# A table of paces with lighter first slots, Gelu ahead of the copy of sums, a tile's end in six pieces, score loads by ScalarE

## The chip, the cores and the metric

One Trainium2 chip, one core of it. The time is the device time of one execution in microseconds; less is better. The kernel before took 4760.69 us in the median of three runs (4751.96 to 4765.37).

## The reference

One layer of an encoder for 1152 tokens (1024 of a prompt, 8 sequences of 16 new ones), all in fp32: normalization and modulation, one input projection, a gated linear attention (gla) and a stick-breaking attention, their merge, a residual with normalization, and then a retrieval of single-neuron experts. The last part takes most of the time:

```python
q = (h @ peer_wq).reshape(n, PEER_HEADS, 2, PEER_HALF)
s = jnp.einsum('nhpd,hpkd->nhpk', q, peer_keys)
sc, ix = lax.top_k(s, PEER_TOPK)                       # 16 of 128, two halves, 8 heads
cand = sc[:, :, 0, :, None] + sc[:, :, 1, None, :]
top, pos = lax.top_k(cand.reshape(...), PEER_TOPK)     # 16 of 256
eid = jnp.take_along_axis(cid, pos, axis=-1)
g = jax.nn.softmax(top, axis=-1)
act = jax.nn.gelu(jnp.einsum('nhkd,nd->nhk', peer_u[eid], h))
return jnp.einsum('nhk,nhkd->nd', g * act, peer_v[eid])
```

Each token picks 128 of 16384 experts, so 1152 x 128 rows of 4 KB are read from `peer_u` and as many from `peer_v`, 1.2 GB in all.

## The kernel before

The 1152 tokens are nine tiles of 128, in three groups of three tiles (`GROUPS`). For each group the program goes through six stages: norm, stick, gla, mix, res, select. Select computes the scores of all three tiles and chooses the experts of the first; the scores of the two others go to DRAM.

Beside the stages, from the select of group 0 on, runs the retrieval (`Peer`), cut into **slots**. There are 128 slots for a tile. In slot s GpSimd fetches one row of `peer_u` for each of the 128 tokens (`fetch_u`, L2424, 0.524 MB, an indirect DMA into one of seven buffers; the first tile alone uses the fourteen of both rings), VectorE multiplies it by the token's vector and sums it (`dot`, L2595), one slot for one expert of every token. A tile later the same tile's values come: for 64 pairs of tokens GpSimd fetches the 128 rows of `peer_v` of each (`fetch_v`, L2432), and TensorE adds a pair with four products (`add_values`, L2494). So the first tile's slots fetch u alone, and from slot 138 on (`FIRST` = 10 in tile 1) both come, about 0.56 pairs a slot. After slot 1151 only values are left.

GpSimd has all fetches in one queue, in order of slots, six slots ahead. Before it fetches it waits until the buffer's last user is done: a dot (VectorE) or a pair (TensorE).

Between a tile's dots and its values lie these steps, at fixed slots k of the next tile: ScalarE's Gelu of the dots (`gelu`, k = 0), VectorE's product with the gates (`weigh`, L2607, `WEIGH_AT` = 2), the transpose of the weights on TensorE (k = 4), ScalarE's copy of it and the spreading of single weights (`set_alone`), and at k = 6 the transpose of the next ids. The sums of the tile before are copied out of PSUM by ScalarE in two halves (`keep_sums`, L2549); the second copy stands behind the last pair, at k = 125, so ahead of the next Gelu in ScalarE's queue. VectorE ends the tile (`finish`, L2613 to L2625) at `END_AT` = 9: gate, residual, normalization, scale and shift, in one go. The experts of the other two tiles of a group are chosen beside the slots (`choose_beside`), from scores that GpSimd loads (`load_beside`, L2291) in two halves; the second load waits until the fourth head is read.

What ties slots to stages is a list that `paces()` computes once: the stages call `K.tick(engine, beside)` at fixed places, 771 times on each of TensorE, VectorE and ScalarE, and the n-th tick runs the engine's part of the retrieval up to slot `slots[n]`. Within a group the slots from `128 * first - 14` up to the next group's are dealt out over its ticks in proportion to a weight for each. In the stick stage two ticks are one step, with one `sb_l` (L1158) and one `sb_z` (L1166) on VectorE.

## Time and profile before

| | us |
|---|---|
| median of three runs | 4760.69 |
| the profiled execution | 4755.65 |
| its span, first to last instruction | 4753.6 |
| TensorE busy | 3429.4 |
| VectorE busy | 2747.8 |
| GpSimd busy (issuing of gathers) | 2400.4 |
| ScalarE busy | 932.0 |

The three runs lie within 0.3% of each other. No single engine is busy throughout, and DMA moved 1580.58 MB at a mean of 333 GB/s. The span falls into five parts: group 0 alone to about 850 us; the select of group 0 and the stick stage of group 1, in which only u rows are fetched, to 1272; the rest of group 1 to 2115; group 2 to 3442; and the tail with the gathers alone. A share of the whole span is a mean over these, so the rows are read by part. A PE clock of 0.50 means 1.2 GHz, of 1.00 2.4 GHz.

### The profile page before, as it was taken

Reading aid. Unit: us, or ns where it says so; the run is one execution under the profiler, and the core shown is the slowest. Engines: PE = TensorE matmul, PEld = TensorE weight load, DVE = VectorE, ACT = ScalarE, POOL = GpSimd, SP = SyncE. Lnnn points to the kernel's source line nnn. Section 1 sums busy time; section 2 is a strip of 40 time slices with the busy share of each in tenths; the row PEclk is TensorE's granted clock in tenths of the full one; section 3 lists DMA queues with packets and bytes.
Section 4 is the critical chain, followed back from the end, with each engine's and each line's share of the span. In section 5 each row is a group of like instructions: output and inputs, shape, how many; then the busy total and the mean of one; then the engine's idle time right before and its main releaser. Section 6 shows DMA issues by size and latency. Waiting matters only on the chain.

```text
span 4753.6 us, 46576 instructions
## 1 busy us (share of the span) xinstructions
PE 3429.4 (72%) x16090; PEld 1698.1 (36%) x16090; DVE 2747.8 (58%) x6580; ACT 932.0 (20%) x2008; POOL 2400.4 (50%) x2390
## 2 busy tenths in 40 slices
PE   7989999878889799778898797897833333333355
PEld 4556754545445443334344364442400000000000
DVE  3443313789777554787776777446866576654420
ACT  3552300134422200114445232000100000000000
POOL 0000000235576555566776666465566666666665
PEclk8999999989998799889999898898955555555566
DMA  8775352678899999999999999899999999999998
GB/s 317 276 252 198 146 165 82 262 270 292 309 362 355 349 381 419 380 399 353 373 383 334 340 356 374 328 419 391 346 377 378 375 388 373 384 357 372 381 374 330
DMA packets 445319, 1580.58 MB, mean 333 GB/s; under 512 B 48328, under 2 KB 87624, under 8 KB 434720
## 3 DMA queue, kind: packets, MB, share of 16 engines
q0 software_dynamic: 342544, 1297.77, 71.2%
q1 hardware_dynamic: 100640, 278.20, 15.9%
q8 instruction: 131, 2.15, 0.2%
q10 hardware_dynamic: 1904, 1.65, 0.1%
q14 instruction: 100, 0.82, 0.0%
HBM read 1527.99 MB, written 49.43 MB: 332 GB/s over the span
## 4 chain that ended last, share of the span: by engine, by line
PE 35%; DVE 19%; POOL 17%; issue 10%; DMA 10%; another core or an unknown queue 6%; ACT 3%; SPq 0%; PEld 0%; DVEq 0%; ACTq 0%; PEldq 0%; POOLq 0%
POOL peer_v_ring L2432 9%; POOL peer_u_ring L2424 7%; PE wide L1829 6%; DVE peer_u_ring L2595 5%; DMA peer_v_ring<-in_peer_v,expertsT 5%; PE wide L750 4%; PE bank L2494 4%; PE wide L2136 3%; PE wide L1401 3%; PE wide L1389 2%; DMA peer_u_ring<-in_peer_u,experts 2%; PE wide L815 2%; PE wide L760 1%; PE wide L796 1%
## 5 line engine op out<-in xcount | busy, mean ns | idle before, releaser
L2424 POOL DMA_INDIRECT peer_u_ring<-in_peer_u,experts x1089 | 1123.3, 1032 | 777.8 <-DVE peer_u_ring L2595 454.3
L2494 PE MATMUL bank<-peer_v_ring,peer_lone 128*32 128x512 f32 x4356 | 805.5, 811 | 888.3 <-DMA peer_v_ring<-in_peer_v,expertsT 705.2
L2432 POOL DMA_INDIRECT peer_v_ring<-in_peer_v,expertsT x1089 | 1096.7, 1007 | 592.0 <-issue 296.5
L2595 DVE SCALAR_TENSOR_TENSOR peer_u_ring<-peer_u_ring,wide 128x1024 f32<-128x1024 f32 x680 | 813.4, 1217 | 486.8 <-DMA peer_u_ring<-in_peer_u,experts 435.5
L2494 PEld LDWEIGHTS bank<-peer_v_ring,peer_lone 128*32 128x32 f32 x4356 | 110.2, 123 | 1440.3 <-issue 1403.6
L2595 DVE SCALAR_TENSOR_TENSOR peer_u_ring<-peer_u_ring,peer_h 128x1024 f32<-128x1024 f32 x409 | 490.7, 1218 | 25.8 <-SPq L271 15.9
L1401 PE MATMUL wide<-w_ring,hT 128*128 128x256 f32 x1152 | 268.2, 391 | 6.9 <-DVE gla_v L1726 6.9
L750 PE MATMUL wide<-hT,w_ring 128*128 128x384 f32 x768 | 267.4, 496 | 5.9 <-DVE sb_hide L2699 3.1
L2136 PE MATMUL wide<-mT,w_ring 128*128 128x384 f32 x768 | 266.1, 496 | 3.1 <-SPq L271 3.1
L2393 POOL MEMSET peer_lone<- 128x1087 f32 x1 | 1.0, 1003 | 488.3 <-SPq L271 488.3
L1401 PEld LDWEIGHTS wide<-w_ring,hT 128*128 128x128 f32 x1152 | 221.5, 195 | 69.8 <-issue 39.2
L1865 DVE TENSOR_TENSOR mix_gate<-mix_gate,wide 128x384 f32<-128x384 f32 x42 | 23.2, 554 | 357.9 <-PE wide L1829 266.3
L1829 PE MATMUL wide<-hT,w_ring 128*128 128x384 f32 x576 | 203.3, 506 | 10.5 <-SPq L271 9.8
L1158 DVE SCALAR_TENSOR_TENSOR sb_l<-sb_z,sb_l 128x768 f32<-128x768 f32 (+2 forms) x120 | 95.5, 796 | 168.8 <-ACT sb_l L1034 165.6
L1166 DVE TENSOR_TENSOR sb_z<-sb_z,wide 128x768 f32<-128x768 f32 (+2 forms) x120 | 95.0, 792 | 163.3 <-PE wide L815 94.9
L2136 PEld LDWEIGHTS wide<-mT,w_ring 128*128 128x128 f32 x768 | 142.3, 192 | 122.0 <-issue 35.8
L825 PE MATMUL wide<-sb_l,before 128*128 128x384 f32 (+2 forms) x384 | 131.2, 467 | 75.3 <-DVE sb_z L1166 61.3
L750 PEld LDWEIGHTS wide<-hT,w_ring 128*128 128x128 f32 x768 | 144.2, 194 | 105.6 <-issue 16.7
L815 PE MATMUL wide<-sb_l,from_here 128*128 128x384 f32 (+2 forms) x480 | 161.2, 460 | 27.4 <-DVE sb_l L1158 24.2
L1829 PEld LDWEIGHTS wide<-hT,w_ring 128*128 128x128 f32 x576 | 111.4, 197 | 105.4 <-issue 28.1
L760 PEld LDWEIGHTS wide<-w_ring,hT 128*128 128x128 f32 x1152 | 139.6, 194 | 17.8 <-issue 9.3
L760 PE MATMUL wide<-w_ring,hT 128*128 128x128 f32 x1152 | 142.4, 278 | 0.0
(312 smaller groups left out, 4901.3 us busy)
## 6 DMA issues: line engine op xcount, KB each, us to landing
w_ring<-in_weights SPq DMA_DIRECT2D x312, 512.0 KB
sb_kc<-in_kcT POOLq DMA_DIRECT2D x16, 2048.0 KB, 7.9
sb_vc<-in_vc POOLq DMA_DIRECT2D x16, 2048.0 KB, 8.7
peer_u_ring<-in_peer_u,experts POOLq DMA_INDIRECT x1089
peer_v_ring<-in_peer_v,expertsT POOLq DMA_INDIRECT x1089
mod_w<-in_w_ada SPq DMA_DIRECT2D x15, 1024.0 KB, 11.0
mod_w_later<-in_w_ada SPq DMA_DIRECT2D x9, 1024.0 KB, 8.0
scores<-sel_sc SPq DMA_DIRECT2D x6, 1024.0 KB
```

The costliest lines, as they stand in the source:

```text
L750: last = pe.matmul(out[:, 0:G.T], w[:, k, :], K.hT[:, k, 0:G.T], start=(k == 0), stop=(k == KC - 1))
L760: last = pe.matmul(out[:, i * P:(i + 1) * P], K.hT[:, k, i * P:(i + 1) * P], w[:, k, :], start=(k == 0), stop=(k == KC - 1))
L815: last = pe.matmul(r[:, h, c0:G.W], K.from_here[:, :], self.l[:, n % self.NL, h, c0:G.W], start=clears, stop=True, skip_group_check=True)
L825: last = pe.matmul(r[:, h, c0:G.W], K.before[:, :], self.l[:, n % self.NL, h, c0:G.W], start=False, stop=True, skip_group_check=True)
L1158: dve.scalar_tensor_tensor(l, self.z[:, n % self.NZ, :, c0:G.W], 0.0, l, ALU.max, ALU.add).then_inc(self.sp_ready, 1)
L1401: last = pe.matmul(out[:, i * DV:(i + 1) * DV], K.hT[:, k, n * P:(n + 1) * P], halves[k // 4][:, k % 4, :], start=(k == 0), stop=(k == KC ...
L1829: last = pe.matmul(out[:, 0:G.T], w[:, k, :], x[:, k, 0:G.T], start=(k == 0), stop=(k == KC - 1))
L2136: last = pe.matmul(out[:, 0:G.T], w[:, k, :], K.mT[:, k, 0:G.T], start=(k == 0), stop=(k == KC - 1))
L2424: pool.indirect_dma_start(buffer, None, K.A["peer_u"], bass.IndirectOffsetOnAxis(ap=K.ids_of[:, j % CHOSEN, k:k + 1], axis=0)).then_inc(lo ...
L2432: pool.indirect_dma_start(buffer, None, K.A["peer_v"], bass.IndirectOffsetOnAxis(ap=K.ids_of_turned[:, j % CHOSEN, t:t + 1], axis=0)).then ...
L2494: last = pe.matmul(self.F.psum[strip:strip + 32, :], self.lone[:, mark - at:mark - at + 32], self.buffer("v", m)[0][:, c * HALF:(c + 1) * ...
L2595: dve.scalar_tensor_tensor(u, u, 1.0, h2, ALU.mult, ALU.mult, accum_out=self.dots[:, j % 2, k:k + 1]).then_inc(self.dot_done, 1)
```

## The change

Eight edits, and no arithmetic is changed.

1. `paces()` deals the slots of a group out not evenly by weight, but so that a slot up to 140 counts 0.6 (`ONLY_U`) and a later one 1. Only group 1 is affected.
2. `K.part(engine, beside, share)` runs a share of the next tick's slots early. VectorE calls it in norm after each tile's sums and in gla after the scans, before the first use of q, before and after the root of a head.
3. In mix VectorE has eight ticks ahead of the first column block, four ahead of the others and none ahead of the last, instead of four ahead of each.
4. The second copy of sums moves from k = 125 to k = `SUMS_AT` = 4 of the next tile, behind Gelu. `WEIGH_AT` is 5 instead of 2, and the transposes follow it.
5. `finish` is a generator of six pieces, run at k = 8, 9, 11, 12, 14 and 15.
6. Values start at k = 12 and end at the same slot; ids are transposed at k = 9.
7. The loads of scores are issued by ScalarE instead of GpSimd, with the same waits.
8. The turns of choosing: 30 instead of 26 for the first tile, loads at (22, 61) and (3, 48) instead of (18, 57) and (4, 51).

The stages of group 1 start at these slots (the ticks' numbers are the same in both):

| stage of group 1 | tick | slot before | slot after |
|---|---|---|---|
| norm | 187 | 16 | 18 |
| stick | 189 | 21 | 25 |
| gla | 279 | 159 | 189 |
| mix | 335 | 237 | 256 |
| res | 399 | 309 | 318 |
| select | 419 | 332 | 337 |
| norm of group 2 | 455 | 374 | 374 |

Slot 138, with the first values, falls on tick 264 before and on tick 244 after. In group 2 both have stick at 379, gla at 553, mix at 628, res at 696, select at 718 and the end at 754.

```diff
+    def part(self, who, beside, share):
+        n = self.ticks[who]
+        was = self.slots[n - 1]
+        return beside.upto(was + math.ceil(share * (self.slots[n] - was)))
...
+    def work(slot):
+        return ONLY_U * min(slot, SLOTS + Peer.FIRST) + max(0, slot - SLOTS - Peer.FIRST)
...
-            out.append(int(before + (to - before) * done / total))
+            while at < to and work(at + 1) - work(before) <= (work(to) - work(before)) * done / total:
+                at += 1
+            out.append(at)
...
-            for _ in range(4):
+            for _ in range(8 if j == 0 else 4 if j + 1 < KC else 0):
                 K.tick("DVE", beside)
...
-    TURNS = ((26, 10, (0, 3, 5, 8), 7, (18, 57)),) + ((10, 12, (0, 3, 6, 9), 8, (4, 51)),) * (TILES - 1)
+    TURNS = ((30, 10, (0, 3, 5, 8), 7, (22, 61)),) + ((10, 12, (0, 3, 6, 9), 8, (3, 48)),) * (TILES - 1)
...
-    WEIGH_AT, END_AT, FIRST, SPAN = 2, 9, 10, 116
-    IDS_AT = (18,) + (6,) * (TILES - 1)
+    SUMS_AT = 4
+    WEIGH_AT, END_AT, FIRST, SPAN = 5, (8, 9, 11, 12, 14, 15), 12, 114
+    IDS_AT = (18,) + (9,) * (TILES - 1)
...
+            self.K.select.load_beside(act, s)
             self.K.select.exp_beside(act, s)
...
-                    if k == self.value_slot(63) + 1:
-                        self.keep_sums(act, j, 1)
+            if j >= 1 and k == self.SUMS_AT:
+                self.keep_sums(act, j - 1, 1)
...
-            if j >= 2 and k == self.END_AT:
-                self.finish(dve, j - 2)
+            if j >= 2 and k in self.END_AT:
+                if k == self.END_AT[0]:
+                    pieces = self.finish(dve, j - 2)
+                next(pieces)
```

VectorE in the stick stage of group 1, before slot 138: `sb_l` and `sb_z` are the stage's, `peer_dots` are dots of one slot each, MAX and the like choose experts. Before, four of the stage's instructions:

```order
L1166 TENSOR_TENSOR sb_z<-sb_z,wide 128x2x256
L2595 SCALAR_TENSOR_TENSOR peer_v_ring,peer_dots<-peer_v_ring,peer_h_155 128x1024
L1158 SCALAR_TENSOR_TENSOR sb_l<-sb_z,sb_l 128x768
L2595 SCALAR_TENSOR_TENSOR peer_v_ring,peer_dots<-peer_v_ring,peer_h_155 128x1024 x2
L2208 MAX peer_top<-peer_wide 128x8 x2
L2211 MAX_INDEX peer_at<-peer_top,peer_wide 128x8 x2
L2213 TENSOR_TENSOR peer_wide<-peer_top 128x256
L1166 TENSOR_TENSOR sb_z<-sb_z,wide 128x768
L2595 SCALAR_TENSOR_TENSOR peer_u_ring,peer_dots<-peer_u_ring,peer_h_155 128x1024
L1158 SCALAR_TENSOR_TENSOR sb_l<-sb_z,sb_l 128x768
L2595 SCALAR_TENSOR_TENSOR peer_u_ring,peer_dots<-peer_u_ring,peer_h_155 128x1024
```

After, two of them in the same part of the stage:

```order
L2624 SCALAR_TENSOR_TENSOR peer_v_ring,peer_dots<-peer_v_ring,peer_h_155 128x1024 x2
L1183 SCALAR_TENSOR_TENSOR sb_l<-sb_z,sb_l 128x768
L2624 SCALAR_TENSOR_TENSOR peer_v_ring,peer_dots<-peer_v_ring,peer_h_155 128x1024
L2237 MAX peer_top<-peer_wide 128x8 x2
L2240 MAX_INDEX peer_at<-peer_top,peer_wide 128x8 x2
L2242 TENSOR_TENSOR peer_wide<-peer_top 128x256
L2624 SCALAR_TENSOR_TENSOR peer_v_ring,peer_dots<-peer_v_ring,peer_h_155 128x1024
L1191 TENSOR_TENSOR sb_z<-sb_z,wide 128x768
L2624 SCALAR_TENSOR_TENSOR peer_v_ring,peer_dots<-peer_v_ring,peer_h_155 128x1024
```

There are now two slots for each of the stage's instructions where before one or two stood.

VectorE at the start of mix of group 2 (`mix_gate` is the stage's first product, which needs TensorE's third product of the stage; `gla_og` and `gla_o` end gla). Before:

```order
L1780 TENSOR_TENSOR gla_og<-gla_og,norm_w 128x768
L1784 SCALAR_TENSOR_TENSOR gla_o<-gla_o,gla_rms,gla_og 128x256 x3
L2595 SCALAR_TENSOR_TENSOR peer_u_ring,peer_dots<-peer_u_ring,peer_h_155 128x1024 x3
L2591 COPY wide<-peer_h_155 128x1024
L2595 SCALAR_TENSOR_TENSOR peer_u_ring,peer_dots<-peer_u_ring,wide 128x1024 x6
L1865 TENSOR_TENSOR mix_gate<-mix_gate,wide 128x384
L2595 SCALAR_TENSOR_TENSOR peer_u_ring,peer_dots<-peer_u_ring,wide 128x1024 x2
L1865 TENSOR_TENSOR mix_gate<-mix_gate,wide 128x384
L1869 TENSOR_TENSOR mT<-mix_gate 128x384
```

After:

```order
L2624 SCALAR_TENSOR_TENSOR peer_u_ring,peer_dots<-peer_u_ring,peer_h_155 128x1024
L1809 TENSOR_TENSOR gla_og<-gla_og,norm_w 128x768
L1813 SCALAR_TENSOR_TENSOR gla_o<-gla_o,gla_rms,gla_og 128x256 x3
L2620 COPY wide<-peer_h_155 128x1024
L2624 SCALAR_TENSOR_TENSOR peer_u_ring,peer_dots<-peer_u_ring,wide 128x1024 x10
L1894 TENSOR_TENSOR mix_gate<-mix_gate,wide 128x384
L2624 SCALAR_TENSOR_TENSOR peer_u_ring,peer_dots<-peer_u_ring,wide 128x1024 x2
L1894 TENSOR_TENSOR mix_gate<-mix_gate,wide 128x384
L1898 TENSOR_TENSOR mT<-mix_gate 128x384
```

Ten dots stand between gla and the first product instead of six, and two of the three that stood behind gla's scaling went ahead of it, with one more right before it.

ScalarE at the end of tile 7, in the tail (`peer_prod` is the copy of sums, `peer_act_v` Gelu, `peer_wT` the copy of the transposed weights). Before:

```order
L2542 ACTIVATE peer_lone<-peer_wT 128x16
L2549 ACTIVATE peer_prod<-bank 64x512 x2
L2523 ACT_TABLE_LOAD
L2523 ACTIVATE peer_act_v<-peer_dots 128x128
L2529 ACTIVATE peer_wT<-bank 128x128
L2542 ACTIVATE peer_lone<-peer_wT 128x16 x5
```

After:

```order
L2570 ACTIVATE peer_lone<-peer_wT 128x16
L2551 ACT_TABLE_LOAD
L2551 ACTIVATE peer_act_v<-peer_dots 128x128
L2577 ACTIVATE peer_prod<-bank 64x512 x2
L2557 ACTIVATE peer_wT<-bank 128x128
L2570 ACTIVATE peer_lone<-peer_wT 128x16 x5
```

The copy of sums went behind Gelu; the rest stands as it stood.

## Rows read from the trace of the kernel before

A row of a view by stretch gives the stretch, its length, then the busy time and the number of instructions of PE, PEld, DVE, ACT and POOL, and last the granted TensorE clock, the DMA share and GB/s.

**Rows 1.** busy by stretch; columns: stretch, length, engines' us, PEclk, DMA, GB/s

```profile
985.00:1272.00 287.00, 259.79 (x1234) 157.35 (x1232) 249.68 (x602) 131.23 (x234) 136.38 (x115) 0.96 0.81 282
1272.00:1345.00 73.00, 44.75 (x200) 14.94 (x200) 49.97 (x126) 19.38 (x34) 55.71 (x50) 0.79 0.99 376
1345.00:1629.00 284.00, 248.32 (x1172) 156.28 (x1165) 205.60 (x535) 73.95 (x228) 191.23 (x166) 0.88 0.94 358
1629.00:1861.00 232.00, 210.96 (x774) 101.27 (x772) 106.29 (x194) 14.27 (x28) 129.95 (x139) 0.95 0.98 388
1861.00:1960.00 99.00, 68.52 (x229) 26.63 (x230) 73.55 (x170) 4.78 (x9) 50.84 (x51) 0.80 0.98 393
1960.00:2115.00 155.00, 125.99 (x548) 61.89 (x546) 118.71 (x400) 19.34 (x51) 83.57 (x89) 0.88 1.00 392
2115.00:2700.00 585.00, 503.15 (x2410) 236.98 (x2407) 413.68 (x922) 256.49 (x415) 404.56 (x364) 0.93 0.96 361
2700.00:2975.00 275.00, 235.54 (x1160) 149.48 (x1162) 196.44 (x501) 74.09 (x228) 175.63 (x161) 0.92 0.93 359
3300.00:3442.00 142.00, 122.99 (x528) 63.28 (x528) 108.59 (x373) 19.56 (x51) 74.15 (x78) 0.92 0.94 358
3442.00:4560.00 1118.00, 383.39 (x1583) 46.91 (x1583) 640.24 (x1458) 26.71 (x85) 751.54 (x800) 0.50 0.97 376
```

**Rows 2.** groups of instructions, VectorE, 950 to 1250 us: busy us, mean ns

```profile
L2595 DVE SCALAR_TENSOR_TENSOR peer_u_ring<-peer_u_ring,peer_h 128x1024 f32<-128x1024 f32 x53 | 63.8, 1219 | 1.3 <-ACTq L271 1.3
L1158 DVE SCALAR_TENSOR_TENSOR sb_l<-sb_z,sb_l 128x768 f32<-128x768 f32 (+2 forms) x31 | 24.3, 782 | 8.8 <-ACT sb_l L1034 8.5 <-issue 0.3
```

**Rows 3.** busy time by stretch, the end of slots without values

```profile
1208.00:1272.00 64.00, 61.91 (x317) 37.36 (x315) 46.51 (x77) 37.22 (x61) 30.23 (x25) 1.00 0.78 266
```

**Rows 4.** timeline, a pair of values; start us, us, engine, line

```profile
2784.60 1.07 PE L2494 MATMUL bank<-peer_v_ring,peer_lone 128*32 128x512 f32 x8
```

**Rows 5.** busy time by stretch, mix of group 0, with no slot beside

```profile
611.00:778.00 167.00, 166.93 (x512) 97.76 (x511) 12.25 (x23) 9.12 (x17) 0.00 (x0) 0.99 0.47 148
```

**Rows 6.** timeline at the ends of two heads of gla, idle before in brackets

```profile
1481.75 0.48 DVE L1689 SCALAR_TENSOR_TENSOR state<-state,gla_decay,wide 128x256 f32<-128x256 f32 x1 [3.15 <-PE wide L1441]
...
1492.16 0.94 POOL L2424 DMA_INDIRECT peer_u_ring<-in_peer_u,experts  x1 [9.04 <-DVE peer_u_ring L2595]
...
2785.41 0.94 POOL L2424 DMA_INDIRECT peer_u_ring<-in_peer_u,experts  x1 [6.96 <-DVE peer_u_ring L2595]
```

**Rows 7.** timeline at the start of mix, group 2

```profile
3014.49 0.55 DVE L1865 TENSOR_TENSOR mix_gate<-mix_gate,wide 128x384 f32<-128x384 f32 x1 [31.73 <-PE wide L1829]
...
3016.96 0.94 POOL L2424 DMA_INDIRECT peer_u_ring<-in_peer_u,experts  x1 [23.88 <-DVE peer_u_ring L2595]
```

**Rows 8.** timeline at the end of tile 7

```profile
4188.75 1.93 PE L2494 MATMUL bank<-peer_v_ring,peer_lone 128*32 128x512 f32 x8 [3.06 <-DMA peer_v_ring<-in_peer_v,expertsT]
...
4202.34 1.19 ACT L2549 ACTIVATE peer_prod<-bank 64x512 f32<-64x512 f32 x2 [82.37 <-remote]
...
4206.88 0.93 POOL L2424 DMA_INDIRECT peer_u_ring<-in_peer_u,experts  x1 [8.16 <-DVE peer_u_ring L2595]
```

**Rows 9.** waits in the tail, 3450 to 4560 us: total us, times, longest

```profile
DVE peer_w L2607 <- ACT peer_act_v L2523: 13.3, 2, 7.9
```

**Rows 10.** busy time by stretch, the end of tile 7

```profile
4195.00:4215.00 20.00, 0.92 (x2) 0.36 (x2) 12.03 (x24) 3.39 (x7) 8.10 (x9) 0.50 0.68 248
```

**Rows 11.** timeline at the end of tile 6, a tile's end on VectorE

```profile
3845.91 1.22 DVE L2613 TENSOR_TENSOR peer_prod<-peer_prod,peer_g 128x1024 f32<-128x1024 f32 x1
...
3849.57 0.94 POOL L2424 DMA_INDIRECT peer_u_ring<-in_peer_u,experts  x1 [0.30 <-issue]
...
3853.91 1.29 DVE L2625 SCALAR_TENSOR_TENSOR peer_x<-peer_x,peer_y,peer_ln 128x1024 f32<-128x1024 f32 x1
```

**Rows 12.** the score loads' line: ns min/median/max, idle before

```profile
L2291 POOL DMA_DIRECT2D peer_sc_half<-scores x12: 567/588/603, 961.6 to 3979.1; - x12
...
  DVE peer_wide L2203: 20.9, 1
```

More of the change, by code:

```diff
@@ L2 @@
 from dataclasses import dataclass
+import math
 import concourse.bass as bass
@@ L471, in vector @@
             n += 3
+            K.part("DVE", beside, (i + 1) / (G.nt + 1))
         dve.wait_ge(self.steps, n)
@@ L1720, in vector @@
             dve.tensor_tensor_scan(c, self.goes_on[:, 1, cols], la, 0.0, ALU.mult, ALU.add).then_inc(self.c_ready, 1)
+            K.part("DVE", beside, 0.5)
             for n in range(1, G.nt):
@@ L1733, in vector @@
                 dve.tensor_tensor(out, x[:, :, NEW - 1:NEW].broadcast_to(x.shape), x, ALU.subtract).then_inc(self.kd_diff_s, 1)
+            K.part("DVE", beside, 0.5)
             q = self.p_bank["q", H]
@@ L2616, in finish @@
         dve.scalar_tensor_tensor(x, x, ALPHA, prod, ALU.mult, ALU.add).then_inc(self.summed, 1)
+        yield
         dve.wait_ge(self.summed, j + 1)
-        n = layer_norm_steps(dve, self.steps, LN_STEPS * j, x, self.small)
+        n = layer_norm_sums(dve, self.steps, LN_STEPS * j, x, self.small)
+        yield
+        n = layer_norm_root(dve, self.steps, n, self.small)
+        yield
         if j == 0:
```

36 lines of the change are left out of this document (22 added, 14 removed).

## The prediction

> **What bounds the kernel now.** I read four views, in this order. First the busy times of the engines by stretch, cut where the stages of the second and third group of tiles begin and end [rows 1]. Its columns for TensorE, VectorE and the DMA share are to be read side by side: the one near 1 is the limit. It shows two regimes. In 985 to 1272 us (the stick stage of group 1, slots 21 to 138, in which only rows of `peer_u` are gathered) DMA works at 0.81 and 282 GB/s; VectorE is busy 249.68 of 287 us (0.87) and TensorE 259.79 (0.91). From 1272 on, when rows of `peer_v` come too, the DMA share is 0.93 to 1.00 with TensorE at 0.61 to 0.91 while the stages last, and 0.97 in the tail (3442 to 4560), where only the gathers run. So the kernel is one long gather with two kinds of loss: DMA idle before 1272 (0.19 of 287, 55 us) and small holes after it. Second, the groups of instructions in the first regime, for the price of one step and one dot on VectorE [rows 2]. Third, the timelines around the holes [rows 6 to 8, 11]: there the reader is to look at the idle time in brackets and at who ended it. Fourth, the loads of the scores [rows 12].
>
> **The new paces, first tile.** The table moves the slots 25 to 189 into the stick stage of group 1 instead of 21 to 159. Up to slot 138 the stage now advances 55 ticks instead of 75; two ticks are one step. A step costs VectorE two instructions of 0.78 us, a dot 1.22 [rows 2], so 10 steps less are 15.6 us less, and 4 dots less 4.9. VectorE's demand falls from 249.7 to 229.2 us. At the share that it had, 0.87, that is 264 us instead of 287: **-23**. The bounds are 229 (VectorE without a gap, -58) and no gain but that of the dots (-5). I stay at the old share because the two engines wait for each other: the last part, 1208 to 1272, where nothing is chosen, has VectorE at 0.73 and TensorE at 0.97 [rows 3], so there the steps are what counts, and 0.87 is the mean of both kinds.
>
> The 20 ticks do not vanish. They took 259.79/75 = 3.46 us of TensorE each, 69 us, and go to where values are added too. The rest of the stick stage now holds 51 slots with values instead of 21. Such slots took 73/21 = 3.48 us here, 284/78 = 3.64 in gla and 585/174 = 3.36 in the next stick stage [rows 1]. I take 3.35, since in the two ends TensorE had also the stage change: 171 us instead of 73, **+98**. The stick stage ends 75 us later than before.
>
> **What comes back.** The later stages of group 1 hold fewer slots: gla 67 instead of 78, mix 62 for 72, res 19 for 23, select 37 for 42, 30 fewer in all. If DMA is the only limit, a slot is two fetches of 0.524 MB, and 30 at 375 GB/s give back 84 us. If TensorE is, a slot gives back 0.56 of a pair of values, 1.07 us each [rows 4]: 0.6 us, 18 in all. Between these, by stage: gla moved 358 GB/s with TensorE at 0.87, and the same stage of group 2, with 75 slots, took 275 instead of 284 (3 us a slot, though its other work differs): I take 1.8 a slot, -20. Mix: 232 us with TensorE 0.91; with no slots at all it took 167 at full TensorE [rows 1, 5]; the mean slope is 0.9 a slot, -10. Res (TensorE 0.69, DMA 0.98): -8. Select (DMA 1.00; 142 us with 36 slots in group 2 against 155 with 42): -10. Together **-48**, bounds -18 and -84. The paces alone thus cost 98 - 23 - 48 = **+27**. From slot 374 on the table is the same. The later turns of the choosing (slot 30 for 26), of the loads and of the transposed ids follow the slots; they change no engine's work, 0.
>
> The Trainium skill, SBUF — State Buffer, section "SBUF: two separate sides", gives about 358 GB/s between HBM and a core. By that figure gla stands at its ceiling and the 30 slots are worth, as an estimate, 88 us. The rows of mix, res and select have 388 to 393 GB/s, so the figure is no ceiling here, and the sum doesn't use it.
>
> **Dots spread in gla, more of them ahead of mix.** At a head's end VectorE has a long run without a dot: waits for TensorE (3.15 us) and ScalarE, thirteen small steps of a root, the scaling. GpSimd, whose queue holds u and v fetches in one order, waits 9.04 us for a dot there, in group 2 6.96 [rows 6]. There are four heads in each of two groups. The change puts one or two dots into the waits; it does not shorten the work: 0 to 3 us for a head, -6 for each group. At the start of mix of group 2 VectorE waits 31.73 us for TensorE (which waits for `mix_oB`), and GpSimd 23.88 us for a dot [rows 7]. Ten dots stand ahead of that wait now instead of six: four slots, 4.2 MB, at most 11 us. I take -7 in group 2 and -2 in group 1, where the longest such wait of VectorE has fewer idle fetches behind it.
>
> **Gelu ahead of the copy of sums, weights three slots later.** At the end of tile 7 the last pair of values ended at 4190.68 by its record, but the copy of sums, in front of Gelu in ScalarE's queue, began at 4202.34, and GpSimd waited 8.16 us for the next dot [rows 8]. VectorE stood that long with the product of weights at its head: 13.3 us in two waits in the tail, the longest 7.9 [rows 9]. DMA was at 0.68 over 20 us [rows 10], against the tail's 0.97: 5.8 us lost at that end, and the other wait adds some 4. With Gelu first the product needs only the dots. What is late next is the copy of sums: the transposes of weights and ids wait for it at slots 7 and 9, and the first pair of values at slot 12. Twelve slots of one dot of 1.22 us are 14.6 us and the copy was 11.7 late, so it is just covered. In the tail **-10** (0 to -13), beside the stages -2 for each of four ends: -8. If it is later than that, TensorE stands at the transpose with the stages' matmuls queued behind it, and ScalarE at the copy with `exp` and the stages' copies behind; the price is what exceeds the 14.6 us.
>
> **A tile's end in six pieces.** It held VectorE 9.3 us in one run (3845.91 to 3855.20), but GpSimd's fetch in the middle of it came 0.30 us behind the one before it [rows 11]: the ring of seven covers it in the tail, 0. Beside the stages of group 2 there are three such runs with main work behind them; -1 each. Without that cover each would cost 9 us, which is what the pieces insure.
>
> **Score loads by ScalarE.** Twelve issues of 0.59 us and a wait of 20.9 us leave GpSimd's queue [rows 12]; the wait lies before 1272, where GpSimd waits for dots anyway: 0. They are now in front of ScalarE's `exp` and of the copies of the stages. A wait there is for a head's choosing that VectorE reaches two slots later at most; bounds 0 and 5 us for each of eight loads beside stages; I take +1 each, **+8**. The Trainium skill, DMA: Bandwidth & Descriptors, "Issuing engines are not separate DMA queues", says that a move to another issuing engine saves only the sequencer's time to issue; by it the gain is those 12 x 0.59 us on GpSimd and no bandwidth, which is what I took.
>
> **Sum:** +27 - 12 - 9 - 18 - 3 + 8 = -7 from the profiled execution's 4755.65, that is 4749. That execution lies 5 us under the median of the three (4760.69), so I say 4749 without adding the 5 in full: **4750**. A difference of 0.3%, 14 us, is about what a measurement of this kernel tells from none: faster means under 4746, slower over 4775.
>
> **Rivals.** (1) *The refund is DMA's price.* If 30 slots give back 84 instead of 48, and VectorE closes its gaps before 1272 a little (another -5), the time is 4708, or 4710 against the median. For it: DMA at 0.98 to 1.00 in three of the four stages. Against: the select of group 2 was at 0.94, gla at 0.93. (2) *Slower: TensorE becomes the bound of group 1's later part.* It is left idle before slot 138 (55 x 3.46 = 190 of 264 us busy) and gets 69 us more between slots 138 and 374, where it had 698.5 of 843 us, 0.83 [rows 1]. If the refund is 22 instead of 48 and the smoothing brings half of its 42, the sum is -7 + 26 + 21 = +40: 4796. It decides from a refund of under 30 us. (3) *ScalarE holds the stages.* A load's wait ahead of the copies of stick and gla costs 5 us eight times, 40 instead of 8: 4782. For it: `exp` already waits so; against: ScalarE is busy 0.06 to 0.46 of these stretches [rows 1]. (4) *The smoothing doesn't do what it says*, since DMA fills the holes later anyway: without the 42 us it is 4791; I count it with (2).
>
> **Chances.** Forecast 0.42 (own range 4736 to 4765), (1) 0.27, (2) with (4) 0.22, (3) 0.09. Faster by over 0.3%: all of (1) and 0.15 of the forecast's, 0.42. Within 0.3%: 0.27 of the forecast's, 0.02 of (3): 0.29. Slower: 0.29. The range that leaves out one in ten on each side is 4706 to 4792.
>
> **What would show it.** The stick stage of group 1 ends near 1420 instead of 1345, and slot 138's dot near 1250. TensorE's share falls to about 0.72 before 1250. Stage select of group 1 ends near 2135 to 2145 against 2115: under 2110 is rival 1, over 2155 rival 2. At the ends of tiles 5 and 7 VectorE no longer waits ahead of the product of weights, and Gelu stands before the copy. GpSimd's wait at the start of mix of group 2 is under 15 us. ScalarE's waits ahead of the loads, if over 3 us in the mean, speak for rival 3. The forecast is wrong if VectorE's share before slot 138 isn't 0.85 to 0.92, since all of the first part is scaled by it.

## The result, and the profile after

The changed kernel took 4719.74 us in the median of six runs (4710.28 to 4735.28), the kernel before 4757.06 (4744.63 to 4767.25): a ratio of 0.9923, with the interval 0.9894 to 0.9952. That is 37 us faster, 0.8%. The forecast was 4750 with a range of 4706 to 4792: the time lies in the range, but under the forecast's own 4736 to 4765. The profiled execution took 4716.24 us, 39.4 less than the one of before.

The busy time by stretch, cut at the stages of the changed kernel. The columns are the stretch, its length, then PE, PEld, DVE, ACT and POOL, the granted TensorE clock, the DMA share and GB/s:

```profile
958.00:989.00 31.00, 5.36 (x26) 4.83 (x27) 25.22 (x60) 5.30 (x11) 11.27 (x12) 0.53 0.72 271
989.00:1224.00 235.00, 189.75 (x857) 115.32 (x858) 227.51 (x571) 89.62 (x164) 137.18 (x107) 0.93 0.87 301
1232.00:1391.00 159.00, 127.00 (x646) 58.43 (x644) 109.92 (x271) 58.37 (x104) 115.26 (x107) 0.93 1.01 395
1391.00:1649.00 258.00, 234.05 (x1132) 150.80 (x1132) 174.69 (x425) 74.48 (x222) 154.13 (x136) 0.91 0.89 336
1649.00:1860.00 211.00, 202.88 (x739) 101.08 (x738) 97.36 (x172) 13.27 (x28) 119.09 (x125) 0.98 0.99 398
1860.00:1950.00 90.00, 62.16 (x208) 23.89 (x208) 65.62 (x157) 4.72 (x9) 44.34 (x42) 0.85 0.92 340
1950.00:2110.00 160.00, 126.81 (x540) 65.24 (x541) 121.47 (x404) 19.36 (x51) 81.58 (x86) 0.87 0.97 377
2110.00:2673.00 563.00, 492.94 (x2386) 235.65 (x2384) 405.36 (x907) 254.93 (x414) 393.02 (x348) 0.96 0.97 365
3405.00:4517.00 1112.00, 383.88 (x1582) 46.90 (x1582) 643.95 (x1474) 24.80 (x82) 758.38 (x799) 0.50 0.97 379
```

They answer to [rows 1]. The second row is the stretch with u rows alone: 235 us where it was 287. VectorE is busy 227.51 of them, 0.97, where it had 0.87; TensorE fell from 0.91 to 0.81; DMA rose from 0.81 to 0.87. The stick stage of group 1 now ends at 1391 instead of 1330, group 1 at 2110 instead of 2118, group 2 at 3405 instead of 3437. So the time by which the changed kernel is ahead is 48 us when the dot of slot 138 ends (1224.1 against 1272.5), 6 when group 2's stick stage begins (slot 379, 2117.6 against 2124.0), 30 at its end (slot 754, 3411.8 against 3441.9) and 39 at the end.

VectorE's waits in the first stretch; columns: the waiting tile and line, what it waited for, us in total, times, the longest. Before:

```profile
DVE sb_z L1166 <- PE wide L815: 21.0, 15, 3.5
DVE sb_l L1158 <- ACT sb_l L1034: 11.8, 12, 3.9
```

After:

```profile
DVE sb_l L1183 <- ACT sb_l L1059: 2.0, 1, 2.0
DVE sb_z L1191 <- PE wide L840: 0.8, 1, 0.8
```

The waits of a step for TensorE and for ScalarE, 33 us in 27 times, are all but gone. TensorE's share was to fall to about 0.72 by the prediction; it fell to 0.81, since the stretch got shorter as well.

### The profile page after: what moved, and what is told of

It is laid out like the page before. It is cut to its first block, busy times and chain, and to the rows that moved or that the text cites. A ratio compares the mean times of both kernels' runs of the same rounds, so it can differ in the third digit from the quotient of the medians.

```text
span 4714.4 us, 46570 instructions
## 1 busy us (share of the span) xinstructions
PE 3409.5 (72%) x16090; PEld 1699.0 (36%) x16090; DVE 2747.0 (58%) x6580; ACT 932.0 (20%) x2007; POOL 2414.7 (51%) x2378
## 4 chain that ended last, share of the span: by engine, by line
PE 42%; DVE 18%; POOL 14%; issue 11%; DMA 8%; another core or an unknown queue 4%; ACT 2%; SPq 0%; DVEq 0%; ACTq 0%; POOLq 0%
PE wide L1858 8%; POOL peer_v_ring L2462 7%; POOL peer_u_ring L2454 6%; PE bank L2522 5%; PE wide L2165 5%; DVE peer_u_ring L2624 5%; DMA peer_v_ring<-in_peer_v,expertsT 4%; PE wide L1426 3%; PE wide L775 3%; PE wide L1414 3%; PE wide L840 2%; PE bank L1858 2%; PE wide L785 1%; DVE peer_v_ring L2624 1%
## 5 line engine op out<-in xcount | busy, mean ns | idle before, releaser
L2454 POOL DMA_INDIRECT peer_u_ring<-in_peer_u,experts x1089 | 1138.8, 1046 | 709.9 <-DVE peer_u_ring L2624 376.3
L2624 DVE SCALAR_TENSOR_TENSOR peer_u_ring<-peer_u_ring,wide 128x1024 f32<-128x1024 f32 x662 | 797.6, 1217 | 578.9 <-DMA peer_u_ring<-in_peer_u,experts 479.5
L2624 DVE SCALAR_TENSOR_TENSOR peer_u_ring<-peer_u_ring,peer_h 128x1024 f32<-128x1024 f32 x427 | 513.2, 1218 | 26.0 <-SPq L283 16.4
```

Source lines behind the costliest of these rows:

```text
L2454: pool.indirect_dma_start(buffer, None, K.A["peer_u"], bass.IndirectOffsetOnAxis(ap=K.ids_of[:, j % CHOSEN, k:k + 1], axis=0)).then_inc(lo ...
L2624: dve.scalar_tensor_tensor(u, u, 1.0, h2, ALU.mult, ALU.mult, accum_out=self.dots[:, j % 2, k:k + 1]).then_inc(self.dot_done, 1)
```

## The experiments

All kernels were timed beside the kernel before on their own chip. The first eight ran on a chip on which the kernel before takes 4607.5 and 4611.7 us (medians of the two sets); it is called the first chip below. The last four ran on one where it takes 4763.0, the second chip; the executions of the result (4757.06) are like those and are set beside them, though the changed kernel was not timed again in that set. So ratios and the times of slots are compared within a chip.

| kernel | median, us | ratio to before | interval |
|---|---|---|---|
| new paces alone | 4602.43 | 0.9986 | 0.9976 to 0.9996 |
| changed, old paces | 4568.38 | 0.9911 | 0.9899 to 0.9924 |
| changed, loads on GpSimd | 4558.91 | 0.9894 | 0.9880 to 0.9908 |
| changed, `ONLY_U` 0.45 | 4579.72 | 0.9933 | 0.9920 to 0.9945 |
| changed, again | 4563.54 | 0.9900 | 0.9884 to 0.9917 |
| changed, no shares, old mix ticks | 4573.65 | 0.9924 | 0.9906 to 0.9942 |
| changed, old end of a tile | 4582.53 | 0.9936 | 0.9917 to 0.9955 |
| second chip: end in one piece | 4735.83 | 0.9949 | 0.9928 to 0.9969 |
| second chip: pieces, old Gelu order | 4726.70 | 0.9931 | 0.9908 to 0.9955 |
| second chip: 0.8, loads on GpSimd | 4714.08 | 0.9902 | 0.9878 to 0.9925 |
| second chip: 0.7, loads on GpSimd, no shares | 4724.41 | 0.9930 | 0.9907 to 0.9953 |

Where the time went is read from the ends of dots in the profiled executions. Length of stretches by slots, us:

| kernel | to 138 | 138 to 379 | 379 to 553 (stick) | 553 to 754 | 754 to end |
|---|---|---|---|---|---|
| before | 1277.8 | 847.6 | 559.4 | 736.2 | 1188.3 |
| new paces alone | 1226.2 | 896.2 | 559.5 | 736.3 | 1187.6 |
| changed | 1227.6 | 880.0 | 546.7 | 716.3 | 1192.4 |
| changed, old paces | 1284.6 | 843.8 | 546.8 | 717.9 | 1190.8 |
| changed, loads on GpSimd | 1225.7 | 887.7 | 544.8 | 713.4 | 1190.3 |
| changed, 0.45 | 1219.7 | 910.8 | 542.3 | 720.0 | 1189.3 |
| changed, no shares | 1220.1 | 887.6 | 544.8 | 726.6 | 1193.2 |
| changed, old end | 1230.5 | 882.2 | 566.0 | 721.8 | 1186.8 |
| second chip: before | 1272.5 | 851.5 | 579.9 | 738.0 | 1311.7 |
| changed | 1224.1 | 893.5 | 568.6 | 725.6 | 1302.6 |
| end in one piece | 1223.4 | 896.3 | 586.7 | 728.1 | 1315.8 |
| pieces, old Gelu order | 1226.9 | 887.2 | 565.0 | 731.2 | 1312.6 |
| 0.8, loads on GpSimd | 1246.6 | 864.3 | 571.2 | 726.6 | 1304.4 |
| 0.7, loads on GpSimd, no shares | 1231.5 | 881.5 | 569.8 | 730.1 | 1304.6 |

All rows from "second chip: before" down are to be read together; before and changed there are the executions of the result. The same stick stage with the same end of a tile took 542.3 to 546.8 us in five kernels of the first chip and 565.0 to 571.2 in four of the second. Each row is one execution, and some of these were the slowest of their kernel: old paces 17 us over its median, end in one piece 17, old end 7, 0.45 4. A row of these kernels can hold that much too much somewhere, so below the place of a loss is read from single steps where it can be.

**The kernel before, for its slots.**

> The kernel before itself, for its milestones on the same chip as the runs beside it. The chip of the four runs so far fetched faster in the tail (slots 754 to 1151 in 1010 us instead of 1116); if this one is like it, the median is near 4607, slot 138 at 1275 to 1285, slot 374 at 2120 to 2128, and group 2's slots 374 to 754 take 1300 to 1310 us, since the new paces alone do not touch them (1303.1 there).

It took 4611.34 us, one execution; slot 138 at 1277.8, slot 374 at 2118.0 (2 us ahead of what was given), group 2 in 1303.0, tail as said.

**New paces alone.** The kernel before with edit 1 and nothing else:

```diff
+    def work(slot):
+        return ONLY_U * min(slot, SLOTS + Peer.FIRST) + max(0, slot - SLOTS - Peer.FIRST)
...
-            out.append(int(before + (to - before) * done / total))
+            while at < to and work(at + 1) - work(before) <= (work(to) - work(before)) * done / total:
+                at += 1
+            out.append(at)
```

> The kernel before with the new paces alone; the loads of scores stay in GpSimd's queue, Gelu and the tile's end stay as they were, no shares of ticks are run early. Theory A (a tight VectorE and a tight TensorE waited for each other in the stick stage of group 1, and fewer stage steps per slot leave VectorE alone as the bound): the dot of slot 138 ends at 1225 to 1232 us instead of 1272.5, VectorE's share ahead of it is 0.94 or more, slot 374 ends 10 to 18 us early, the whole 4738 to 4746. Theory B (the load's wait of 20.9 us at the head of GpSimd's queue was what held the stretch, and it is the move of the loads to ScalarE that freed it): slot 138 at 1245 to 1255, VectorE at 0.87 to 0.90, the whole 4755 to 4780. Theory C (the shares of ticks run early close the gaps): as B.

Slot 138's dot ended at 1226.2, with the loads still in GpSimd's queue and no shares of ticks: theory A's mark, and B and C fall. The whole was 4602.43, 0.14% faster. The totals of this and the next three expectations are on the scale of the result's chip; A's 4738 to 4746 is 11 to 19 us under the 4757 of before. It was 5 under, and slot 374 came 3 us early and not 10 to 18. So the gain ahead of slot 138 was as A says and more of it was given back. The stretch up to slot 138 in this kernel:

```profile
990.00:1226.00 236.00, 189.88 (x851) 114.29 (x851) 228.38 (x574) 88.91 (x163) 140.62 (x111) 0.92 0.85 308
```

**Changed, with the old paces.**

```diff
-CHOSEN, ONLY_U = 4, 0.6
+CHOSEN, ONLY_U = 4, 1.0
```

> The changed kernel with a first-tile slot counting 1 instead of 0.6, so with the table of before; all other edits stay. Theory A: slot 138 at 1262 to 1273, the whole 4728 to 4736 (what the edits behind slot 374 bring, 24 us, is kept). Theory B: slot 138 at 1245 to 1255 with VectorE's share up, since ScalarE issues the loads here too, and the whole 4705 to 4722. Theory C: as B, slot 138 under 1255.

Slot 138 ended at 1284.6, later than A's 1273 (the kernel before has 1277.8 on this chip), and the whole was 39 us under before (41 by the ratio), where A had 21 to 29. The stretch and VectorE's waits in it are like those of before, although ScalarE issues the loads here:

```profile
994.00:1284.00 290.00, 262.07 (x1236) 159.83 (x1235) 250.50 (x601) 131.92 (x235) 135.98 (x113) 0.95 0.82 278
DVE sb_z L1191 <- PE wide L840: 23.6, 18, 3.5
DVE sb_l L1183 <- ACT sb_l L1059: 13.4, 12, 6.7
```

What the paces are worth inside the changed kernel is 4568.38 - 4563.54 = 5 us by medians, and 5 by the ratios, as much as they are alone; the two intervals overlap.

**Changed, with the loads of scores on GpSimd.** The three waits and the transfer of `load_beside` are GpSimd's again:

```diff
-        act.dma_start(self.sc_half[...], ...)
+        pool.dma_start(self.sc_half[...], ...)
...
-            self.K.select.load_beside(act, s)
...
+            if s >= 0:
+                K.select.load_beside(pool, s)
```

> The changed kernel with the loads of scores back in GpSimd's queue, at the same turns. Theory A: slot 138 at 1222 to 1230 as in the changed kernel (1224.1), the whole within 6 us of it (4713 to 4725); my prediction priced the move at +8, by which it would be 4708 to 4714. Theory B: slot 138 at 1240 to 1255, the whole 4730 to 4745.

Slot 138 at 1225.7 and 4558.91 us: B falls here too. Against the changed kernel (4563.54) it is 4.6 us faster, but the two were timed in different sets, in which the kernel before took 4607.5 and 4611.7; by the ratios it is 3 us, and the intervals overlap. The move is worth nothing, or costs a little. No gain of edit 7 shows. In the changed kernel each load takes ScalarE's queue a third of a microsecond, and no idle time stands ahead of it that the view names:

```profile
L2320 ACTq DMA_DIRECT2D peer_sc_half<-scores x12: 326/327/353, 961.0 to 3919.1; - x12
```

**A first-tile slot that counts 0.45.**

```diff
-CHOSEN, ONLY_U = 4, 0.6
+CHOSEN, ONLY_U = 4, 0.45
```

> The changed kernel with a first-tile slot counting 0.45 instead of 0.6: slot 138 falls on tick 231 instead of 242, 11 ticks earlier. Theory A: VectorE is the bound already and stays at 0.96 to 0.98, so the stretch falls only by its own work, 11 ticks of 0.79 us and 3 dots of 1.22: 12 us, slot 138 at 1210 to 1214; behind it each tick costs 1.3 to 1.5 us (the changed kernel spent 875 us from slot 138 to 374 with 213 ticks, the one before 842 with 189), +15. The whole 4712 to 4724. If TensorE were still what the stretch waits for, it would fall by 11 ticks of 3.4 us, 37 us, slot 138 at 1187, the whole 4695.

Slot 138 came at 1219.7, 8 us earlier than with 0.6 (1227.6), where 12 were expected and 37 would have spoken for TensorE as the limit. The stretch behind it grew by 31 us instead of 15, 2.8 us a tick; the whole was 16 us slower than with 0.6, where 8 less to 4 more was expected. The stretch ahead of slot 138 with 0.45, and with 0.8 (the kernel further below, on the second chip):

```profile
997.00:1219.00 222.00, 158.05 (x664) 96.29 (x665) 215.85 (x554) 69.70 (x133) 130.50 (x103) 0.86 0.86 295
```

```profile
991.00:1246.00 255.00, 219.54 (x1045) 134.45 (x1044) 235.53 (x582) 112.55 (x203) 139.12 (x112) 0.96 0.84 296
```

With the rows above they make a series. The weight of a slot going 1.0, 0.8, 0.6, 0.45, TensorE's share goes 0.90, 0.86, 0.81, 0.71, and VectorE's 0.86, 0.92, 0.97, 0.97. The less TensorE is near its limit, the fewer gaps VectorE has; below 0.6 there is hardly a gap left to close.

**The changed kernel again.**

> The changed kernel, timed beside the runs that leave a part out. Ratio to before 0.989 to 0.993. If the move of the loads to ScalarE costs what the prediction says (+8 us), it is 4 to 12 us slower than with the loads on GpSimd (ratio 0.9894 on record), so 0.991 to 0.992; if it costs nothing, 0.989.

4563.54 us, ratio 0.9900: the gain of the result is there on the other chip too, 1.0% instead of 0.8%. The ratio lies between the 0.989 that was given for loads that cost nothing and the 0.991 to 0.992 for loads at the prediction's price, and tells neither.

**No shares of ticks, old ticks ahead of mix.** Edits 2 and 3 undone:

```diff
-        return beside.upto(was + math.ceil(share * (self.slots[n] - was)))
+        return beside.upto(was)
...
-            for _ in range(8 if j == 0 else 4 if j + 1 < KC else 0):
+            for _ in range(4):
```

> The changed kernel without shares of ticks run early and with VectorE's four ticks ahead of each column block of mix, as before. Theory P (the holes at a head's end in gla and at the start of mix are what the remaining 25 us of group 2 come from): slots 374 to 754 take 1290 to 1303 us instead of 1280, and the whole is 15 to 30 us slower than the changed kernel. Theory G (it is the tile's end: Gelu ahead of the copy, six pieces): within 6 us of the changed kernel. The prediction's terms say 21 of 42 us: 18 to 24 slower.

10 us slower, where the prediction's terms had 21, theory P 15 to 30 and theory G at most 6; the intervals overlap a little. The mark of P, slots 374 to 754 in 1290 to 1303 us, isn't met: 1278.9, against 1281.6 in the changed kernel, whose dot of slot 374 the shares bring forward by 11 us and that of 379 not at all. From 379 on the loss is there: 553 to 754 takes 726.6 instead of 716.3 us, while the stick stage before it is not touched. It lies in mix, slots 628 to 696, 228.1 instead of 214.8 us, of which 3.3 had been gained in gla. The idle time (in brackets) of GpSimd ahead of its first fetch behind mix's first product; in the changed kernel:

```profile
2986.04 0.94 POOL L2454 DMA_INDIRECT peer_u_ring<-in_peer_u,experts  x1 [7.18 <-DVE peer_u_ring L2624]
```

Without edits 2 and 3:

```profile
2956.76 0.94 POOL L2454 DMA_INDIRECT peer_u_ring<-in_peer_u,experts  x1 [23.81 <-DVE peer_u_ring L2624]
```

In the last kernel of the table, which keeps the ticks of mix but not the shares:

```profile
2988.12 0.93 POOL L2454 DMA_INDIRECT peer_u_ring<-in_peer_u,experts  x1 [17.42 <-DVE peer_u_ring L2625]
```

The 23.81 us answer to the 23.88 of [rows 7]. The eight ticks alone take 6 us off the wait, the shares ahead of them another 10. What the wait lost isn't all gain: in the changed kernel GpSimd also waits 7.16 and 2.64 us for TensorE's pairs shortly ahead of it, where the kernel before has one such wait of 2.44.

**The old end of a tile.** Edits 4 to 6 undone: the copy of sums ahead of Gelu at k = 125, weights at 2, the end in one piece at 9.

```diff
-    SUMS_AT = 4
-    WEIGH_AT, END_AT, FIRST, SPAN = 5, (8, 9, 11, 12, 14, 15), 12, 114
-    IDS_AT = (18,) + (9,) * (TILES - 1)
+    WEIGH_AT, END_AT, FIRST, SPAN = 2, 9, 10, 116
+    IDS_AT = (18,) + (6,) * (TILES - 1)
```

> The changed kernel with the tile's end of before: the second copy of sums ahead of Gelu, weights at slot 2, the end of a tile in one piece at slot 9. Theory P: within 8 us of the changed kernel. Theory G: 15 to 30 us slower, most of it at slots 384 to 400, 512 to 530 and 640 to 660 of group 2, and some 10 us in the tail. The prediction's terms say 21: 10 in the tail, 11 beside stages.

19 us slower, with intervals that just touch: the largest part of the change. But not where the prediction put it: the profiled execution, 7 us over its median, has 25 us more in group 2 (566.0 for 546.7 in stick, 721.8 for 716.3 behind it), and its tail is 5.6 us *faster* with the old end. All three kernels with the old end on this chip have 1186.8 to 1188.3 there, the five with the new one 1189.3 to 1193.2.

**Which half of it.** The next two split the end, on the second chip.

```diff
-                    pieces = self.finish(dve, j - 2)
-                next(pieces)
+                    for _ in self.finish(dve, j - 2):
+                        pass
```

> The changed kernel with a tile's end on VectorE in one piece at slot 8; the copy of sums stays behind Gelu. The tile's end as a whole was worth 25 us in slots 379 to 754 and nothing in the tail. Theory G1 (the gain is Gelu and the product of weights: VectorE no longer stands for ScalarE and TensorE no longer for the transposes): 0 to 5 us slower than the changed kernel (4564 to 4569 on this chip). Theory G2 (the gain is the six pieces: 9.3 us in which VectorE does no stage work, three times in group 2): 15 to 25 us slower, 4578 to 4588. My prediction gave 3.

Its counterpart has the old constants of the run above but for `END_AT` = (9, 10, 11, 12, 14, 15), and the old place of the copy.

> The changed kernel with the copy of sums ahead of Gelu and weights at slot 2 as before, but the end of a tile in six pieces at slots 9 to 15. It is the counterpart of the run beside it. Theory G1: 15 to 25 us slower than the changed kernel, 4578 to 4588, like the run with all of the old end (4582.5). Theory G2: 4564 to 4569.

Against the 0.9923 of the changed kernel in the result, one piece gives 0.9949 and the old Gelu order 0.9931, 12 and 4 us; both differences are within the intervals. So the kernel with pieces is where theory G2 had it, and one piece lies short of G2's 15 to 25 and over G1's 0 to 5. The steps of the stick stage are clearer than the totals. Two ends of a tile lie in it (slots 393 and 521). Five steps about each, from one `sb_z` to the fifth after it and both ends together, against all the rest of the stage, us:

| kernel | tile's end | steps about the two ends | rest of the stage |
|---|---|---|---|
| before | one piece | 94.6 | 464.8 |
| changed | six pieces | 82.6 | 464.1 |
| changed, old end | one piece | 96.0 | 470.0 |
| second chip: before | one piece | 95.8 | 484.2 |
| changed | six pieces | 86.0 | 482.5 |
| end in one piece | one piece | 92.6 | 494.1 |
| pieces, old Gelu order | six pieces | 86.2 | 478.8 |

All nine kernels with pieces, of either Gelu order, have 82.6 to 86.2 there, and the five with an end in one piece 92.6 to 96.0. So the pieces are what the stick stage gained from, and Gelu's order is not; what the changed kernel gained on the kernel before in this stage (12.7 and 11.4 us) lies at the two ends but for 1 to 2 us. The 18 and 19 us by which the stage is longer with the end alone undone are another matter: 6.6 and 13.4 of them are at the ends, the rest in single steps all over executions that were slow as a whole. The steps of the stage on VectorE about the end of tile 2, in one piece (start, us; the end goes from L2643 to L2661):

```profile
2577.77 0.95 DVE L1191 TENSOR_TENSOR sb_z<-sb_z,wide 128x768 f32<-128x768 f32 x1 [2.03 <-PE wide L840]
...
2585.29 0.95 DVE L1191 TENSOR_TENSOR sb_z<-sb_z,wide 128x768 f32<-128x768 f32 x1 [2.82 <-PE wide L840]
...
2588.45 1.22 DVE L2643 TENSOR_TENSOR peer_prod<-peer_prod,peer_g 128x1024 f32<-128x1024 f32 x1
...
2596.41 1.28 DVE L2661 SCALAR_TENSOR_TENSOR peer_x<-peer_x,peer_y,peer_ln 128x1024 f32<-128x1024 f32 x1
2597.61 0.95 DVE L1183 SCALAR_TENSOR_TENSOR sb_l<-sb_z,sb_l 128x768 f32<-128x768 f32 x1
...
2601.65 0.95 DVE L1191 TENSOR_TENSOR sb_z<-sb_z,wide 128x768 f32<-128x768 f32 x1 [1.94 <-PE wide L840]
```

In the changed kernel:

```profile
2572.06 0.95 DVE L1191 TENSOR_TENSOR sb_z<-sb_z,wide 128x768 f32<-128x768 f32 x1 [2.81 <-PE wide L840]
2575.22 1.22 DVE L2643 TENSOR_TENSOR peer_prod<-peer_prod,peer_g 128x1024 f32<-128x1024 f32 x1
...
2579.84 0.95 DVE L1191 TENSOR_TENSOR sb_z<-sb_z,wide 128x768 f32<-128x768 f32 x1 [0.25 <-PE wide L840]
...
2587.35 0.95 DVE L1191 TENSOR_TENSOR sb_z<-sb_z,wide 128x768 f32<-128x768 f32 x1 [0.29 <-PE wide L840]
...
2598.30 0.96 DVE L1191 TENSOR_TENSOR sb_z<-sb_z,wide 128x768 f32<-128x768 f32 x1 [0.74 <-PE wide L840]
2600.32 1.28 DVE L2661 SCALAR_TENSOR_TENSOR peer_x<-peer_x,peer_y,peer_ln 128x1024 f32<-128x1024 f32 x1
```

From one `sb_z` to the next are 7.5 us just ahead of the end. In one piece the step with the end takes 16.4 (2585.29 to 2601.65), 8.9 more. In pieces four steps hold it, of 7.8, 7.5, 10.9 and 8.9 us (2572.06 to 2607.18), 5 over four times 7.5: the waits of 2 to 3 us for TensorE are down to 0.3 to 0.7, so the pieces in part take the place of waits that the stage has anyway. By the table, which takes in the steps behind the end as well, an end in one piece is 3 to 7 us dearer than one in six, as a mean of the two. The third end beside group 2 (slot 649) lies in mix, where VectorE is busy less than half the time, and shows no cost: slots 628 to 696 took 212.4 us with the old end and 214.8 with the new.

**Gelu ahead of the copy, in the tail.** With the old order on the second chip, VectorE waited ahead of the product of weights in the tail as in [rows 9]; here the kernel with pieces alone (total, times, longest):

```profile
DVE peer_w L2635 <- ACT peer_act_v L2550: 9.5, 2, 7.9
```

On the first chip the kernel before has no such wait in its tail: the copy of sums was on time at each end. Here tile 7's (`peer_prod`, the copy, 0.1 us behind the record of the last pair, then Gelu):

```profile
4104.69 1.19 ACT L2549 ACTIVATE peer_prod<-bank 64x512 f32<-64x512 f32 x2 [64.72 <-PE bank L2494]
4105.90 1.28 ACT L2523 ACT_TABLE_LOAD   x1
4107.20 0.31 ACT L2523 ACTIVATE peer_act_v<-peer_dots 128x128 f32<-128x128 f32 x1
```

In the profiled execution of the result the copy was late at this end, and now behind Gelu:

```profile
4157.35 0.31 ACT L2551 ACTIVATE peer_act_v<-peer_dots 128x128 f32<-128x128 f32 x1 [75.34 <-issue]
4176.90 1.19 ACT L2577 ACTIVATE peer_prod<-bank 64x512 f32<-64x512 f32 x2 [19.24 <-issue]
```

The last pair of values before it ended at 4155.6 by its record, 21 us earlier. GpSimd's fetches went on through that time, but the wait has only moved: the first piece of the tile's end, at slot 8, needs the copy too. VectorE stood 8.85 us in front of that piece and began it as the copy ended (4176.90 and 1.19 us):

```profile
4178.13 1.23 DVE L2643 TENSOR_TENSOR peer_prod<-peer_prod,peer_g 128x1024 f32<-128x1024 f32 x1 [8.85 <-issue]
```

DMA in the 20 us while the copy was late, in the 12 behind it, and in the 40 from the last pair on; below, the 40 that answer to these in the kernel before:

```profile
4155.00:4175.00 20.00, 0.58 (x4) 0.00 (x0) 14.03 (x24) 0.31 (x1) 13.89 (x16) 0.50 1.02 413
4178.00:4190.00 12.00, 4.59 (x18) 0.96 (x18) 11.42 (x28) 0.71 (x4) 6.81 (x7) 0.50 0.73 244
4155.00:4195.00 40.00, 7.11 (x30) 1.19 (x26) 30.45 (x60) 2.11 (x6) 26.09 (x28) 0.50 0.93 360
4190.00:4230.00 40.00, 7.08 (x30) 1.05 (x26) 30.29 (x58) 3.39 (x7) 22.94 (x24) 0.50 0.84 318
```

So at this end the new order brought 0.09 of 40 us, an estimate of 3.6 us, and not the whole loss. Where the copy is on time, the first chip's tail is 4 to 6 us longer with the new end over its five ends, about 1 us each. Whether Gelu's order does that or the values that start two slots later isn't shown: the one kernel that undoes it there undoes all of edits 4 to 6. On the second chip the tail from slot 754 took 1302.6 to 1304.6 us in the three kernels with both halves of the new end, 1311.7 and 1312.6 in the two with the old Gelu order, and 1315.8 with Gelu first and the end in one piece. That last kernel shows the same wait at its longest. At the end of tile 6 the copy began 26.0 us behind the record of the last pair, and the whole of the tile's end stood behind it, at slot 8:

```profile
DVE peer_prod L2643 <- ACT peer_prod L2577: 13.1, 1, 13.1
```

**Two candidates.** The first has `ONLY_U` = 0.8 and the loads on GpSimd, the second 0.7, the loads on GpSimd and no shares of ticks:

```diff
-CHOSEN, ONLY_U = 4, 0.6
+CHOSEN, ONLY_U = 4, 0.8
```

> A candidate: the changed kernel with the loads of scores back on GpSimd and a first-tile slot counting 0.8. Theory A (VectorE is the bound from about 0.8 on, each tick moved behind slot 138 costs 1.3 to 1.5 us): slot 138 at 1238 to 1246, 16 us later than with 0.6, and 13 ticks fewer behind it, 17 to 20 us less; the whole 4552 to 4562, level with 0.6 (4558.9). If the optimum were sharp at 0.6 it would be over 4565.

The numbers for this and the next were given for the first chip; both ran on the second, this one at 0.9902. Slot 138 ended at 1246.6, 22.5 us later than with 0.6 (16 expected), and the stretch to slot 379 took 29 less (17 to 20 expected): level, as theory A has it. The tables between 0.6 and 1.0 end close to each other, and only 0.45 is clearly slower.

> A candidate: loads on GpSimd, a first-tile slot counting 0.7, no shares of ticks run early, but the eight ticks ahead of mix kept. Leaving out both the shares and the mix ticks cost 10 us, with no loss before mix of group 2 (slots 379 to 628 took 811 us against 816). If the mix ticks are what is worth the 10 us, the whole is 4550 to 4560; if the shares are, 4564 to 4570.

0.9930, slower than either reading had it, though its interval takes in the changed kernel's 0.9923; against the kernel with 0.8 it is 13 us slower, and those intervals overlap too. By stretch, slots 553 to 696, gla and mix of group 2, took 504.8 us in the kernel before on that chip, 491.3 with the eight ticks alone and 486.4 in the changed kernel. So by one execution each some 5 of the 10 us are the shares' and the rest the ticks', in the same place; the totals don't tell them apart. The best ratios are those of the changed kernel with its loads on GpSimd (0.9894, and 0.9902 with 0.8), but their intervals take in the changed kernel's own: no version was shown to beat it.

## Why the prediction came out as it did

The time lies in the stated range, but the range ran from 51 us faster to 35 slower than the 4757 of before. The sum had -7 us, and the two profiled executions differ by -39; faster by more than 0.3% had been given a chance of 0.42. So that the range holds owes much to its width, and what follows is about the terms.

**The first stretch, -23: right in its work, wrong in its share.** The demand of VectorE was worked out as 229.2 us; with the paces alone it was 228.4. But I divided it by 0.87, the share of before, and gave as a reason that the two engines wait for each other. That reason was right and spoke against the number. In [rows 1] both are near their limits (0.91 and 0.87), and that is when they wait for each other, 33 us in 27 waits; with 12 steps fewer TensorE has slack, and the waits go away with it. The measured share is 0.97, and up to slot 138 the kernel gained 51.6 us (paces alone) where I had 23; the stretch took 236 us, close to my lower end of 229. The mark that I set for this, a share outside 0.85 to 0.92, is the one that failed. A part is a miscount: slot 138 falls on tick 266 before and 242 after, 24 ticks less, not the 20 of the text (264 and 244); by the same working that makes VectorE's demand 3 us less and TensorE's 14.

**The rest of group 1, +98 - 48 = +50: right as a sum.** With the paces alone slots 138 to 374 took 888.9 us instead of 840.2, +48.7. The terms were near: the part of the stick stage with values (slots 138 to 189) took 170.1 us where I had 171, and in the kernel before (138 to 159) 66.8 where I had 73, so +103 for +98, and the rest gave back 55 where I had 48. In the changed kernel mix took 211 us where I had 222, res and select 250 where I had 236. So the paces alone are not +27 but -3 at slot 374 (2115.1 against 2118.0), and -5 as a whole. Rival 1's time (4708 to 4710) is nearer to the 4719.74 than the forecast's, but its mechanism isn't what happened: a refund at DMA's price would have left 14 us in this stretch, not 49.

**Edits 2 and 3, -21: right in kind, half the size.** 10 us, in mix and not in gla: slots 553 to 628 took 269.4 us with the shares and 266.1 without, and in group 1 both kernels are at slot 379 at the same time (2107.6 and 2107.7). The -12 for the heads of gla is the term that failed: with the shares no stretch of gla got shorter. The 10 us lie where the mix term, -9, put them, but it takes the shares as well as the ticks to get them. "Ten dots instead of six" is a misreading of the lines of VectorE's order: behind gla's last instruction nine dots stood before (three and six), and ten stand there now. The four more are right, as 637 dots ahead of mix's first product in group 2 instead of 633; three of them went ahead of gla's scaling, which is the shares' work and not the ticks'. GpSimd's wait fell to 7.18 us, under the 15 that I set as a mark.

**Gelu's order, -18, and the six pieces, -3: the sum right (19 us), the parts exchanged.** The tail's -10 rested on two waits of one execution [rows 8, 9]; they come in some ends and some executions only, and on the first chip, where the kernel before has none, the tail is 4 to 6 us longer with the new end. The term also left out a user of the copy: I gave it the 14.6 us up to slot 12 for cover, but the tile's end needs it at slot 8, after eight dots, 9.8 us, and there VectorE waited 8.85 us for it in the result's own execution. The pieces I priced by the fetches that pass in the middle of a tile's end [rows 11], and took a ring of seven buffers for cover; the work without cover is not the fetches but the stick stage's own step, which stood still for 8.9 us. I had named "main work behind them" and then gave it 1 us an end; 5 to 6 us at each of the two ends in the stick stage is what the changed kernel gained there, and at the end in mix nothing shows. What the rest of the 19 us is stays open.

**The loads on ScalarE, +8:** +3 to +5 measured, within its bounds and not told from none. Rival 3 fell: no wait of ScalarE ahead of a load shows. Rivals 2 and 4 fell with the 39 us at the end.

**The sum.** By medians the parts are, each undone alone: paces -5, smoothing -10, tile's end -19, loads +5, together -29 of the 46 to 48 us by which the changed kernel is ahead on that chip. The rest isn't placed; each of the parts has an uncertainty of several us. Part of it may be the paces: the kernel with the old ones ran from 4563 to 4586 us, and by its profiled execution, the slowest of the five, they would be worth 21 us inside the changed kernel instead of 5. By stretches the gain lies in slots up to 379 (18 us, of which the kernel with the paces alone has 3) and in group 2 (33 us, of which undoing the smoothing gives back 8 and the old end 25), less 4 in the tail.

## What to carry to other kernels

When two engines that feed each other are both near 0.9, neither's share is a constant: here a quarter less work for TensorE and a tenth less for VectorE let VectorE close its gaps from 0.87 to 0.97, so price such a move at the bound engine's demand and not at its share alone. A long run on an engine that a main stage also steps through can cost the stage nearly its full length (8.9 of 9.3 us in its own step here), however well its own consumers are buffered; cut it into pieces that fit the waits that the stage has anyway. A wait seen at two ends of one execution is priced by how often it comes, not by how long it was; and when a late step is moved back, the first of all its users sets how late it may be.
